# Splitting each streamed weight slot into its high and low parts with one instruction of 1024 columns per engine instead of two of 512

## The chip, the cores and the metric

One NeuronCore of a Trainium2 chip runs the whole program. The metric is the device time of one execution in microseconds (us), as the median of several executions of the same program on the same inputs. Lower is better. Engines are named as in the profile: PE is TensorE (the matmuls), PEld its weight loads, DVE is VectorE, ACT is ScalarE, POOL is GpSimd, SP is SyncE, whose queue issues the weight loads.

## The reference

A two layer trunk over 512 latent tokens and 256 context tokens of width 1024, batch 1. Both layers share the same frame:

```python
hl = rmsnorm(x, norm_g[i]) * (1.0 + sc_l) + sh_l        # modulation from silu(c) @ ada_w[i]
# layer 0 (also for the context tokens)
u, z = split(h @ w_in, 2)                               # (tokens, 1024) @ (1024, 4096)
y = fft2(u grouped by 256 features, axes=(tokens, features), norm='ortho').real
x = x + gate * ((y * silu(z)) @ w_out)                  # (tokens, 2048) @ (2048, 1024)
# layer 1, four heads, latent and context tokens
q, k, v, z = split(h @ w_in)                            # q, k rotated for the latent tokens
o = forward + backward retention (decayed scores, state from the context)
x = x + gate * ((rms(o) * silu(z)) @ w_out)
return rmsnorm(x, final_g)
```

Everything is float32.

## The kernel before, in words

**Precision and the split.** Each float32 operand a of a large matmul is used as two numbers: a high part, which is a copy of a into the type fp32r, and a low part, a minus the high part. A product is then three matmuls, high by high, high by low and low by high (`mm3`, lines 1541 to 1543), added in PSUM. So each weight must be split before PE can use it: ACT writes the high part (`hi`, line 662), DVE the low part (`lo`, line 1003).

**The stream.** All large weights lie in DRAM in the order of their use, in slots of 128 by 1024 float32 numbers (512 KB). SP loads them into `raw`, two or three buffers by stage. `ring` holds the split form and has two slots: slot r goes to `ring[:, r % 2]`, its high part at index 0, its low part at index 1.

**The protocol around a slot, half by half.** A slot has two halves of 512 columns. Three counters tie the engines together, each counting two per slot:
- `slot_done` is counted up by PE after the last matmul that reads a half. ACT waits for it before it overwrites this half with the high part of the slot after next.
- `hi_done` is counted up by ACT for each half; DVE waits for it.
- `split_done` is counted up by DVE for each half; PE waits for it (`split`) ahead of the first matmul that reads the half, and SP waits for both halves of a slot before it loads into that slot's `raw` buffer again.

So as soon as PE has finished half 0 of slot r-2, ACT and DVE can split half 0 of slot r, while PE works on half 1.

**Order.** There is no scheduler. Each engine executes one instruction list in order, written out by hand, in which `hi` and `lo` stand between the other work of that stage. A waiting instruction holds up all that follows it on its engine.

**Stages that use `hi` and `lo`**, 96 slots in all:
- z (16 slots of 48 matmuls): the gate projection of layer 0. Between them DVE takes dot products with the streamed modulation weights (line 1035) and POOL multiplies the gates (line 585). The slots of stage u before it are split by `fold_hi` and `fold_lo`, which the change leaves as they are.
- out0 (16 slots of 48): the output projection of layer 0, then the norm of layer 1, where DVE makes 1/rms (1321, 1343), scales (1328) and takes low parts of the activations (1334).
- four heads of 12 slots, s0 to s11: s0, s1 are q, s2, s3 and s6, s11 are z, s4, s5 are k, s7 to s10 are v. Within a head DVE rotates q and k (1393) from PSUM into `turn`, POOL adds up pairs of these (633, 635), ACT and DVE split the sums (893, 1397). DVE and ACT also split v out of PSUM (926, 1449), and the last head's output is normed (1351, 1358) and gated by POOL (625) between the next head's first slots.
- out1 (16 slots of 24): the output projection of layer 1.

On ACT and DVE, `used(s)` in the function `head` is the split of slot s+2, so `used(1)` splits s3 and `used(2)` splits s4. For heads 1 to 3 DVE's order begins

```python
used(0)
o_rstd(h - 1)
used(1)
turns(0, 0, 1)
o_norm(h - 1, 0, 2)
part_lo(1, ...); part_lo(2, ...)
o_norm(h - 1, 2, 4)
used(2)
```

and ahead of s7 PE waits for `turned` and `qklo`, both counted by DVE's work on k, which stands behind `used(5)`, the split of s7. Ahead of s11 PE waits for `vlo`: its PSUM bank 0 holds a tile of v until DVE has taken the low part of it (1449). This stands behind `used(10)`, the split of the next head's s0.

Of the kernel before, what the change touches and what calls it, by code (L numbers as in the profile page):

```python
# [30 lines left out]
ALU = mybir.AluOpType  # L31
ACT = mybir.ActivationFunctionType
# [19 lines left out]
SLOT = 1024  # L52
# [22 lines left out]
DONE0 = 4  # L75
# [12 lines left out]
def raw_at(phase, n):  # L88

    _, bufs, first, before = PHASES[phase]  # L90
    buf = (n + first) % bufs
    return buf, 16 * (before[buf] + n // bufs + 1)


def raw_step(phase, per_iteration):

    return 16 * (per_iteration // PHASES[phase][1])
# [58 lines left out]
def build(nc, x_lat, x_ctx, x_rows, small_in, cond_in, decay_in, stream, tables_in, middle_in,  # L156
          middle_w_in, rope_in, out):
    ctx = ExitStack()
    with ctx:
        def sb(name, shape, dt=F32):  # L160
            return ctx.enter_context(nc.sbuf_tensor(name, shape, dt))

        def sem(name):
            return ctx.enter_context(nc.semaphore(name))


        ring = sb("ring", [P, 2, 2, SLOT], F32R)
# [6 lines left out]
        raw = sb("raw", [P, RAW_BUFS, SLOT])  # L174
# [20 lines left out]
        def f32(ap):  # L195
            return ap.bitcast(F32)
# [129 lines left out]
        hi_done, split_done, slot_done = sem("hi_done"), sem("split_done"), sem("slot_done")  # L326
# [327 lines left out]
        def _(act):  # L654
            def hi(phase, n, r, i=0, per=0):

                buf, landed = raw_at(phase, n)
                act.wait_ge(s_raw[buf], raw_step(phase, per) * i + landed if per else landed)
                for a in range(2):
                    c = slice(a * SLOT // 2, (a + 1) * SLOT // 2)  # L660
                    act.wait_ge(slot_done, 2 * r + (a + 1 - 4 + DONE0))
                    act.activation(ring[:, n % 2, 0, c], raw[:, buf, c], ACT.Copy).then_inc(hi_done, 1)  # L662

            def fold_hi(n):

# [79 lines left out]
            for g in range(GROUPS):  # L745
                if g >= 1:
                    u_hi(g - 1)
                if g >= 2:
                    copy_q(g - 2)
                if g < GROUPS - 1:  # L750
                    fold_hi(2 * g + 2)
                    fold_hi(2 * g + 3)
                else:
                    hi("z", 0, SLOT_Z)
                    hi("z", 1, SLOT_Z + 1)
                if g == 0:
                    act.wait_ge(mid_mm, 1)
                    act.activation(mid_s[0][0:GROUPS, :], bank(7, NF, parts=GROUPS),
                                   ACT.Copy).then_inc(mid_s_hi, 1)
                    act.wait_ge(rstd_row_mm, 1)  # L760
                    act.activation(rstd0, banks[:, 4 * 512:4 * 512 + TOK], ACT.Copy).then_inc(rstd_row, 1)
# [12 lines left out]
            def gates(jj, q, split=None, first=False, last=False):  # L774

                j = 2 * jj + q
                if split is not None:
                    act.wait_ge(gated, 8 * split + 8)
                    for half in range(2):
                        act.activation(g0_hi_at(2 * split + half), one(gate0, 2 * split + half),  # L780
                                       ACT.Copy).then_inc(ghi, 1)
                if last:
                    hi("out0", 0, RING_OUT0)
                    hi("out0", 1, RING_OUT0 + 1)
                else:
                    hi("z", Z_PER * q + 4, 2 * j + (SLOT_Z + 2), jj, 2 * Z_PER)
                    if first:
                        copy_q(GROUPS - 1)
                    hi("z", Z_PER * q + 7, 2 * j + (SLOT_Z + 3), jj, 2 * Z_PER)
                for half in range(2):  # L790
                    for a, b, src in ((0, LAT, bank(3 * q + half)),
                                      (LAT, TOK, bank(3 * q + 2, CTX, CTX * half))):
                        kk = 2 * j + half if split is not None else gate0_at(2 * j + half)
                        act.activation(one(gate0[:, :, a:b], kk), src, ACT.Silu).then_inc(z_done, 1)  # L794
# [193 lines left out]
        def _(dve):  # L988
# [8 lines left out]
            def lo(phase, n, r):  # L997

                buf = raw_at(phase, n)[0]
                for a in range(2):  # L1000
                    c = slice(a * SLOT // 2, (a + 1) * SLOT // 2)
                    dve.wait_ge(hi_done, 2 * r + (a + 1))
                    dve.tensor_tensor(ring[:, n % 2, 1, c], raw[:, buf, c],  # L1003
                                      f32(ring[:, n % 2, 0, c]), ALU.subtract).then_inc(split_done, 1)

            def fold_diff(n):

# [188 lines left out]
            for g in range(GROUPS):  # L1196
                if g < GROUPS - 1:
                    fold_diff(2 * g + 2)
                    fold_diff(2 * g + 3)
                if g >= 1:  # L1200
                    u_lo(g - 1)
                if g >= 2:
                    sum_diff(g - 2)
                if g < GROUPS - 1:
                    fold_lo(2 * g + 2)
                    fold_lo(2 * g + 3)
                else:
                    lo("z", 0, SLOT_Z)
                    lo("z", 1, SLOT_Z + 1)
                if g == 0:  # L1210
                    dve.wait_ge(mid_s_hi, 1)
                    dve.tensor_tensor(mid_s[1][0:GROUPS, :], bank(7, NF, parts=GROUPS),
                                      f32(mid_s[0][0:GROUPS, :]), ALU.subtract).then_inc(mid_s_lo, 1)
# [8 lines left out]
            def gates(jj, q, split=None, first=False, last=False):  # L1222
# [20 lines left out]
                if last:  # L1243
                    dot(2, 4)
                    dot(3, 5)
                    keep_dots(j + EARLY, Z_PER * j + (SLOT_Z + 5))
                    lo("out0", 0, RING_OUT0)
                    lo("out0", 1, RING_OUT0 + 1)
                else:
                    lo("z", Z_PER * q + 4, 2 * j + (SLOT_Z + 2))  # L1250
                    dot(2, 5)
                    dot(3, 6)
                    keep_dots(j + EARLY, Z_PER * j + (SLOT_Z + 6))
                    lo("z", Z_PER * q + 7, 2 * j + (SLOT_Z + 3))
# [744 lines left out]
```

## Time and profile before

| what | value |
|---|---|
| median of 3 runs | 1000.4 us |
| those runs | 1000.3, 1000.4 and 2994.8 us |
| the profiled execution's own time | 998.61 us |
| its span, first to last instruction | 996.8 us |
| mean granted TensorE clock | 0.978 of full speed |
| PE busy | 941.6 us, 94% of the span |
| DVE busy | 562.2 us, 56% |
| ACT busy | 343.6 us, 34% |
| POOL busy | 248.3 us, 25% |
| bytes moved | 98.67 MB, 99 GB/s on average |

The profiled execution is 1.8 us (0.2%) below the median of the timed ones, and 1.8 us of it lie outside the span. PE's 94% is a mean over all stages; the busy share alone doesn't tell where it waits or how near to waiting it is.

### The profile page before, as it was taken

What the parts mean: (1) busy time and instruction counts of PE and PEld (TensorE: products, weight loads), DVE (VectorE), ACT (ScalarE), POOL (GpSimd) and SP (SyncE); (2) the same over time, 40 slices, a digit from 0 to 9 for tenths busy, and PEclk for the clock granted to TensorE, in tenths of its full rate; (3) what the DMA queues carried; (4) which work ended last, traced back from release to release, by engine and by line L of the source; (5) the groups of instructions that cost most, each with busy time, mean ns of one, the idle gap of its engine ahead of it and who ended that gap; (6) DMA issues with size and microseconds to landing.
All of it is one profiled execution on the core that took longest, in us unless ns stands there. A gap on an engine that the chain in (4) does not pass through costs nothing.

```text
span 996.8 us, 12904 instructions
## 1 busy us (share of the span) xinstructions
PE 941.6 (94%) x4748; PEld 810.4 (81%) x4748; DVE 562.2 (56%) x804; ACT 343.6 (34%) x577; POOL 248.3 (25%) x244
## 2 busy tenths in 40 slices
PE   6969998999999999959999999999999999998993
PEld 6968998888888888847888888887888788877882
DVE  6485877899995332358334445426434544565344
ACT  7233334232314332334333334323333323452230
POOL 3337970475574000024100131013100410020001
PEclk9989999999999999989999999999999999998997
DMA  8473332555555211211221122202121121102212
GB/s 307 140 233 152 121 101 90 190 191 173 186 188 206 92 64 64 84 42 56 72 76 52 35 72 69 68 13 84 63 65 40 42 84 42 63 1 89 101 63 84
DMA packets 27864, 98.67 MB, mean 99 GB/s; under 512 B 3848, under 2 KB 4008, under 8 KB 27568
## 3 DMA queue, kind: packets, MB, share of 16 engines
q1 hardware_dynamic: 25792, 90.25, 27.1%
q0 software_dynamic: 2032, 7.89, 2.1%
q8 instruction: 24, 0.39, 0.2%
q14 instruction: 16, 0.13, 0.0%
HBM read 96.01 MB, written 2.10 MB: 98 GB/s over the span
## 4 chain that ended last, share of the span: by engine, by line
PE 87%; DVE 7%; DMA 2%; POOL 2%; ACT 1%; issue 1%; DVEq 0%; SPq 0%; POOLq 0%
PE banks L1541 28%; PE banks L1542 28%; PE banks L1543 27%; DMA raw<-stream 2%; PE banks L1594 2%; DVE hreg L1334 1%; POOL gate L625 1%; DVE xreg L1393 1%; DVE gate L1328 1%; DVE ring L1003 1%; DVE xreg L1533 0%; DVE gate L1358 0%; POOL gate L618 0%; POOL xreg L635 0%; PE banks L1783 0%
## 5 line engine op out<-in xcount | busy, mean ns | idle before, releaser
L1541 PE MATMUL banks<-hreg,ring 128*128 128x512 f32 (+2 forms) x928 | 334.1, 360 | 26.9 <-DVE hreg L1334 9.1
L1542 PE MATMUL banks<-hreg,ring 128*128 128x512 f32 (+2 forms) x928 | 331.8, 358 | 0.0
L1543 PE MATMUL banks<-hreg,ring 128*128 128x512 f32 (+2 forms) x928 | 329.2, 355 | 0.0
L1003 DVE TENSOR_TENSOR ring<-raw,ring 128x512 fp32r<-128x512 f32 x192 | 139.9, 745 | 271.5 <-ACT ring L662 270.8
L662 ACT ACTIVATE ring<-raw 128x512 fp32r<-128x512 f32 x192 | 119.3, 630 | 386.6 <-PE banks L1543 304.7
L1541 PEld LDWEIGHTS banks<-hreg,ring 128*128 128x128 f32 x928 | 176.6, 190 | 55.4 <-issue 12.8
L1543 PEld LDWEIGHTS banks<-hreg,ring 128*128 128x128 f32 x928 | 176.1, 190 | 23.3
L1542 PEld LDWEIGHTS banks<-hreg,ring 128*128 128x128 f32 x928 | 176.6, 190 | 22.3 <-issue 1.0
L585 POOL TENSOR_TENSOR gate<-xreg,gate 128x257 f32<-128x257 f32 (+1 forms) x64 | 76.1, 1219 | 74.0 <-ACT gate L794 57.9
L1035 DVE CUSTOM_DVE_ANT_0 dist<-raw,gate 128x1024 bf16<-128x1024 f32 x64 | 85.8, 1341 | 3.8
L618 POOL TENSOR_TENSOR gate<-gate 128x512 f32<-128x512 f32 x12 | 16.8, 1397 | 250.7 <-ACT gate L868 249.9
L1541 PE MATMUL banks<-ring,hreg 128*128 128x512 f32 x192 | 74.7, 389 | 0.0
L1542 PE MATMUL banks<-ring,hreg 128*128 128x512 f32 x192 | 74.7, 389 | 0.0
L1543 PE MATMUL banks<-ring,hreg 128*128 128x512 f32 x192 | 74.7, 389 | 0.0
L1541 PE MATMUL banks<-wreg 128*128 128x512 f32 (+2 forms) x192 | 72.4, 377 | 0.0
L1543 PE MATMUL banks<-wreg 128*128 128x512 f32 (+2 forms) x192 | 71.9, 375 | 0.0
L1542 PE MATMUL banks<-wreg 128*128 128x512 f32 (+2 forms) x192 | 71.9, 374 | 0.0
L1542 PE MATMUL banks<-wreg,ring 128*128 128x512 f32 (+2 forms) x168 | 58.5, 348 | 0.0
L1543 PE MATMUL banks<-wreg,ring 128*128 128x512 f32 (+2 forms) x168 | 58.1, 346 | 0.0
L1541 PE MATMUL banks<-wreg,ring 128*128 128x512 f32 (+2 forms) x168 | 57.8, 344 | 0.0
L1541 PEld LDWEIGHTS banks<-ring,hreg 128*128 128x128 f32 x192 | 36.0, 188 | 7.5
L1542 PEld LDWEIGHTS banks<-ring,hreg 128*128 128x128 f32 x192 | 36.0, 188 | 7.5
(205 smaller groups left out, 1117.5 us busy)
## 6 DMA issues: line engine op xcount, KB each, us to landing
raw<-stream SPq DMA_DIRECT2D x160, 512.0 KB, 3.3
gate<-x_rows SPq DMA_DIRECT2D x6, 512.0 KB, 6.8
gate<-x_lat POOLq DMA_DIRECT2D x1, 2048.0 KB, 9.5
xreg<-x_lat POOLq DMA_DIRECT2D x1, 2048.0 KB, 10.9
out<-xreg SPq DMA_DIRECT2D x5, 256.0 KB, 2.7
gate<-cond_in POOLq DMA_DIRECT2D x2, 512.0 KB, 4.9
gate<-x_ctx POOLq DMA_DIRECT2D x1, 1024.0 KB, 12.1
xreg<-x_ctx POOLq DMA_DIRECT2D x1, 1024.0 KB, 13.7
```

The costliest lines, as they stand in the source:

```text
L585: pool.tensor_tensor(g, y, g, ALU.mult).then_inc(gated, 1)
L618: pool.tensor_tensor(head_rstd, head_rstd, p_f[:, i % 2, :], ALU.add).then_inc(oacc, 1)
L625: pool.tensor_tensor(g, g, p_f[:, i % 2, :], ALU.mult).then_inc(ogated, 1)
L662: act.activation(ring[:, n % 2, 0, c], raw[:, buf, c], ACT.Copy).then_inc(hi_done, 1)
L1003: dve.tensor_tensor(ring[:, n % 2, 1, c], raw[:, buf, c], f32(ring[:, n % 2, 0, c]), ALU.subtract).then_inc(split_done, 1)
L1035: dve.tensor_tensor_reduce(out=dot_out, in0=raw[:, buf, :], in1=cond_rows[:, v, :], scale=1.0, scalar=0.0, op0=ALU.mult, op1=ALU.add, accu ...
L1328: dve.tensor_tensor(tmp_t[:, k, 0:LAT], tmp_t[:, k, 0:LAT], rstd_t[:, 0:LAT], ALU.mult).then_inc(t_vec, 1)
L1334: dve.scalar_tensor_tensor(out=h_lo[:, k, a:b], in0=tmp_t[:, k, a:b], scalar=mod1[:, 8 + k, v:v + 1], in1=f32(h_hi[:, k, a:b]), op0=ALU.ad ...
L1541: pe.matmul(out, left[0], right[0], start=start, stop=False)
L1542: pe.matmul(out, left[0], right[1], start=False, stop=False)
L1543: return pe.matmul(out, left[1], right[0], start=False, stop=stop)
L1594: last = pe.matmul(o, raw[:, buf, P * k:P * k + P], csf[:, k:2 * KT:KT], start=k == 0, stop=k == KT - 1)
```

## The change

ACT's copy and DVE's subtraction for a streamed slot each become one instruction over all 1024 columns. ACT waits until PE has read both halves of the slot after which this place in the ring comes free, and counts `hi_done` up by two. DVE waits for both, and counts `split_done` up by two. PE's waits, SP's waits, the loads and the slots of stage u are as before.

```diff
                 buf, landed = raw_at(phase, n)
                 act.wait_ge(s_raw[buf], raw_step(phase, per) * i + landed if per else landed)
-                for a in range(2):
-                    c = slice(a * SLOT // 2, (a + 1) * SLOT // 2)
-                    act.wait_ge(slot_done, 2 * r + (a + 1 - 4 + DONE0))
-                    act.activation(ring[:, n % 2, 0, c], raw[:, buf, c], ACT.Copy).then_inc(hi_done, 1)
+                act.wait_ge(slot_done, 2 * r + (2 - 4 + DONE0))
+                act.activation(ring[:, n % 2, 0, :], raw[:, buf, :], ACT.Copy).then_inc(hi_done, 2)
...
                 buf = raw_at(phase, n)[0]
-                for a in range(2):
-                    c = slice(a * SLOT // 2, (a + 1) * SLOT // 2)
-                    dve.wait_ge(hi_done, 2 * r + (a + 1))
-                    dve.tensor_tensor(ring[:, n % 2, 1, c], raw[:, buf, c],
-                                      f32(ring[:, n % 2, 0, c]), ALU.subtract).then_inc(split_done, 1)
+                dve.wait_ge(hi_done, 2 * r + 2)
+                dve.tensor_tensor(ring[:, n % 2, 1, :], raw[:, buf, :], f32(ring[:, n % 2, 0, :]),
+                                  ALU.subtract).then_inc(split_done, 2)
```

## Rows read from the trace of the kernel before

**Rows 1.** The page: busy time of each engine; the chain that ended last, by engine.
```profile
PE 941.6 (94%) x4748; PEld 810.4 (81%) x4748; DVE 562.2 (56%) x804; ACT 343.6 (34%) x577; POOL 248.3 (25%) x244
...
PE 87%; DVE 7%; DMA 2%; POOL 2%; ACT 1%; issue 1%; DVEq 0%; SPq 0%; POOLq 0%
```

**Rows 2.** Waits of PE: for whom, us in total, times, longest.
```profile
PE banks L1541 <- DVE hreg L1334: 9.1, 4, 7.9
...
PE banks L1541 <- DVE ring L1003: 7.6, 5, 4.4
PE banks L1541 <- DVE hreg L1219: 2.6, 1, 2.6
```

**Rows 3.** The two edited lines by source: ns minimum/median/maximum of one; 1024-column forms elsewhere.
```profile
L662 ACT ACTIVATE ring<-raw x192: 614/632/645, 151.9 to 968.0; 128x512 fp32r<-128x512 f32 x192
...
L1003 DVE TENSOR_TENSOR ring<-raw,ring x192: 626/692/1776, 152.6 to 968.7; 128x512 fp32r<-128x512 f32 x192
...
L690 ACT ACTIVATE wreg<-gate x5: 1042/1043/1057, 12.5 to 21.2; 128x1024 fp32r<-128x1024 f32 x5
...
L1092 DVE TENSOR_TENSOR wreg<-gate,wreg x5: 1212/1218/1218, 16.1 to 26.2; 128x1024 fp32r<-128x1024 f32 x5
```

**Rows 4.** Timeline, head 1, slots s3 and s4: start, us, instruction, [idle before].
```profile
569.51 0.63 ACT L662 ACTIVATE ring<-raw 128x512 fp32r<-128x512 f32 x1 [2.10 <-PE banks L1543]
...
570.18 0.69 DVE L1003 TENSOR_TENSOR ring<-raw,ring 128x512 fp32r<-128x512 f32 x1 [0.17 <-ACT ring L662]
570.79 2.48 DVE L1393 TENSOR_TENSOR xreg<-banks,gate 128x512 f32<-128x512 f32 x4
...
573.34 1.30 POOL L633 TENSOR_TENSOR xreg<-xreg 128x512 f32<-128x512 f32 x1 [10.08 <-DVE xreg L1393]
...
575.34 2.81 DVE L1397 TENSOR_TENSOR wreg<-xreg,wreg 128x512 fp32r<-128x512 f32 x2 [0.88 <-ACT wreg L893]
...
579.34 0.69 DVE L1358 TENSOR_TENSOR gate<-banks,gate 128x512 f32<-128x512 f32 x1 [0.59 <-POOL gate L625]
579.94 2.85 DVE L1003 TENSOR_TENSOR ring<-raw,ring 128x512 fp32r<-128x512 f32 x2
...
579.25 1.30 POOL L625 TENSOR_TENSOR gate<-gate 128x512 f32 x1
...
580.50 1.74 POOL L625 TENSOR_TENSOR gate<-gate 128x512 f32 x1
...
581.15 0.50 PE L1541 MATMUL banks<-hreg,ring 128*128 128x512 f32 x1 [0.80 <-DVE ring L1003]
```

**Rows 5.** Timeline, head 0 to head 1, around slot s11.
```profile
528.48 0.69 DVE L1003 TENSOR_TENSOR ring<-raw,ring 128x512 fp32r<-128x512 f32 x1 [3.33 <-ACT ring L662]
529.09 2.48 DVE L1449 TENSOR_TENSOR wreg<-banks,wreg 128x512 fp32r<-128x512 f32 x4
...
530.33 0.39 PE L1541 MATMUL banks<-hreg,ring 128*128 128x512 f32 x1
```

**Rows 6.** Timeline, head 0, around slot s7.
```profile
490.38 0.69 DVE L1003 TENSOR_TENSOR ring<-raw,ring 128x512 fp32r<-128x512 f32 x1 [3.45 <-ACT ring L662]
...
493.71 0.41 DVE L1397 TENSOR_TENSOR wreg<-banks,wreg 128x256 fp32r<-128x256 f32 x1
...
494.97 0.39 PE L1541 MATMUL banks<-ring,hreg 128*128 128x512 f32 x1
```

**Rows 7.** Timeline, the start of stage z; a window behind it, PEclk after POOL.
```profile
158.87 0.69 DVE L1003 TENSOR_TENSOR ring<-raw,ring 128x512 fp32r<-128x512 f32 x1 [1.38 <-ACT ring L662]
...
162.53 0.47 PE L1541 MATMUL banks<-hreg,ring 128*128 128x512 f32 x1 [2.60 <-DVE hreg L1219]
...
162.60:166.00 3.40, 3.40 (x20) 2.96 (x21) 3.40 (x5) 3.40 (x6) 0.00 (x0) 1.00 0.02 5
```

**Rows 8.** Timeline, the first slot of out0.
```profile
296.69 1.16 ACT L662 ACTIVATE ring<-raw 128x512 fp32r<-128x512 f32 x2 [12.02 <-DMA raw<-stream]
...
297.42 1.29 DVE L1003 TENSOR_TENSOR ring<-raw,ring 128x512 fp32r<-128x512 f32 x2 [0.71 <-ACT ring L662]
...
299.12 0.40 PE L1541 MATMUL banks<-wreg,ring 128*128 128x512 f32 x1
```

**Rows 9.** Timeline, from out0 to head 0, and slot s2 of head 0.
```profile
434.50 0.63 ACT L819 ACTIVATE gate<-xreg 128x512 f32<-128x512 f32 x1 [0.16 <-DVE xreg L1289]
...
460.98 0.68 DVE L1003 TENSOR_TENSOR ring<-raw,ring 128x512 fp32r<-128x512 f32 x1
...
461.72 0.50 PE L1541 MATMUL banks<-hreg,ring 128*128 128x512 f32 x1 [0.73 <-DVE ring L1003]
```

**Rows 10.** Timeline, from head 3 to out1; then a window at the next stretch: PEclk is after POOL.
```profile
899.30 1.28 DVE L1003 TENSOR_TENSOR ring<-raw,ring 128x512 fp32r<-128x512 f32 x2
...
900.03 0.80 PE L1541 MATMUL banks<-hreg,ring 128*128 128x512 f32 x1 [4.42 <-DVE ring L1003]
...
900.00:905.00 5.00, 4.97 (x12) 3.95 (x13) 4.19 (x7) 0.04 (x1) 0.00 (x0) 0.50 0.60 191
```

**Rows 11.** Timeline, last slot of out1; then the page's DMA issues, us to landing.
```profile
968.66 0.69 DVE L1003 TENSOR_TENSOR ring<-raw,ring 128x512 fp32r<-128x512 f32 x1 [1.97 <-ACT ring L662]
...
973.23 0.39 PE L1541 MATMUL banks<-hreg,ring 128*128 128x512 f32 x1
...
raw<-stream SPq DMA_DIRECT2D x160, 512.0 KB, 3.3
```

## The prediction

> **What bounds the kernel now.** I read the page first: PE is busy for 94% of the span and holds 87% of the chain that ended last [rows 1]. ACT and DVE, the two engines that the change edits, have half their time and more to spare, so nothing that merely shortens their work shows in the total. The second view is the list of PE's waits: in the part of the run that the change touches, PE waits for DVE's work on activations, for 7.6 us in five places for a split slot, and for 2.6 us at the start of stage z [rows 2]. The third is the timeline around each of these places, and around those where PE only just doesn't wait. The question is no longer how much ACT and DVE do, but how soon after PE lets go of a half the next instruction behind the split can run.
>
> **The price of one slot.** A half costs ACT 0.632 us and DVE 0.692 us; the same operations at 1024 columns, from the start of this kernel, cost 1.043 and 1.218 [rows 3]. So the change takes 2 x 0.632 - 1.043 = 0.22 us per slot from ACT and 2 x 0.692 - 1.218 = 0.17 us from DVE, 21 and 16 us over 96 slots. Most of that is overlap of neighbouring instructions anyway: back to back, DVE starts one every 0.61 us (570.18 to 570.79 in [rows 4]), so I take 1.218 - 0.08 = 1.14 us for the whole against 1.22 for two. The saving in sequence is then 0.08 us per slot. All of this is beside PE's matmuls, and I cost it at nothing.
>
> What counts is the handover. Let PE have read half 1 of slot r-2, and ACT start at once. Before, half 0 has long been split, and DVE is free for its next work 0.63 + 0.04 + 0.61 = 1.28 us after ACT's start (569.51, 570.18, 570.79 in [rows 4]; 0.04 us is the semaphore between them). After, it is free 1.04 + 0.04 + 1.14 = 2.22 us after it. So whatever stands behind a split that waits for PE comes 0.94 us later on DVE, and 1.04 - 0.63 = 0.41 us later on ACT. And where PE waits for half 0 alone, it now waits for 1.21 instead of 0.68 us of DVE.
>
> In most of the 96 slots this is covered: PE has a whole slot of at least 24 matmuls between its release and its first read of slot r. In stage out1, where slots are shortest, both halves are ready at 969.35 and read from 973.23, a cover of 3.88 us [rows 11]; after the change 2.9 would be left. The cover fails at these places:
>
> - **s4 of heads 1 to 3.** PE's release of s1 lets ACT start at 569.51. ACT and DVE split half 1 of s3, and right behind this DVE turns q; then POOL adds, ACT and DVE split q, DVE norms the last head's output in step with POOL's gating, and only then splits s4, for which PE already waits 0.80 us today [rows 4]. Every link follows the one before at once, so 0.94 us go through to the split of s4: it starts at 580.88. At that time POOL's third gating (579.26 to 580.56 before) will still run, and the fourth follows it. In these rows DVE's first half ends at 581.10, 0.54 us after the end of the third, though it started at 579.94, and the second at 582.79, 0.55 us after the end of the fourth. So I take it that the whole waits for the end of the third, at 580.56 + 0.94 = 581.50, and then needs 0.54 + 0.53 = 1.07 us: 582.57, and PE goes at 582.62 instead of 581.15. That is 1.47 us per head, 4.4 for three. The bounds are 1.0 us (a whole of 1.22 us without a collision) and 2.6 (both collisions stay, 2.85 us), so 3.0 to 7.8.
> - **s11 of all four heads.** DVE splits half 1 of the next head's s0 at 528.48 and starts on v at 529.09; PE needs the first low part of v, which ends 0.68 later at 529.77, before s11 at 530.33 [rows 5]. 0.56 us of cover against 0.94 of delay, and 0.04 for the semaphore: 0.42 per head, 1.7 in all. Bounds 1.4 and 2.0.
> - **s7 of all four heads.** Here k's work stands behind the split of s7, and ends at 493.71 + 0.41 = 494.12; PE goes on at 494.97 [rows 6]. Cover 0.85, delay 0.94, semaphore 0.04: 0.13 per head, 0.5 in all, between 0 and 1.0.
> - **Start of z.** DVE's split of the second slot stands ahead of its work on u and of the first low part of h, for which PE waits until 162.53 [rows 7]. No cover: 0.95 us. The bounds are 0.8 and 1.0.
> - **First slot of out0.** ACT starts on the landing of the load at 296.69, DVE ends at 298.71 and PE reads at 299.12 [rows 8], without waiting. After, the split ends 1.04 + 0.04 + 1.22 = 2.30 us after ACT's start, at 298.99, which would still do. But DVE is filled up through stage z, and two splits there, whose high part comes only at PE's release, would hold it 0.4 us longer, and the load with it. 0.3 us, between 0 and 0.7.
> - **From out0 to head 0.** ACT's copy for s1 ends 0.41 us later, at 434.75, and the first square of the last tile, on the way to 1/rms, starts then instead of 434.50: 0.27 us [rows 9]. Then s2: DVE reaches it at 460.98 with its high part ready, and PE goes at 461.72, after half 0. After, it goes after the whole, 1.218 - 0.68 = 0.53 us later. Together 0.8, between 0.5 and 1.0. What is late next is DVE's turn of q in head 0, and this is not late: the two splits ahead of it fill DVE either way.
> - **Third slot of out1.** The same: DVE comes to it at 899.30, PE goes at 900.03 [rows 10]: 0.5 us, between 0.4 and 0.7.
>
> SP's queue waits for the end of both halves before and after, so its loads start 0.94 us later where the split waits for PE; its loads land in some 3.3 us [rows 11], ahead of ACT's next wait for PE in out0, out1 and the heads. I cost this at nothing; if that cover were gone it would be up to 0.9 us per slot.
>
> The sum: 4.4 + 1.7 + 0.5 + 0.95 + 0.3 + 0.8 + 0.5 = 9.2 us, with ends at 6.1 (3.0 + 1.4 + 0 + 0.8 + 0 + 0.5 + 0.4) and 14.2 (7.8 + 2.0 + 1.0 + 1.0 + 0.7 + 1.0 + 0.7). The profiled execution took 998.61 us, so it becomes 1007.8. The median of the runs is 1000.4, 1.8 above it; by the same sum it becomes 1009.6.
>
> A port shared by DVE and POOL is what these rows suggest for s4. The Trainium skill states this as a rule (page SBUF — State Buffer, section Who interferes with whom): a VectorE instruction with two SBUF inputs contends with a GpSimd one that reads SBUF, and whoever comes first holds the pair for its whole instruction. By that rule DVE waits once, for the third gating, and s4 costs the 1.47 us that I took; were there no such rule it would be 1.0, and the sum 7.8 us.
>
> **The rivals.**
>
> *Fewer instructions win, the covers hold.* The saved 0.08 us of sequence per slot would count wherever DVE is the bound, and if DVE's 0.94 us were absorbed in the links to s4 (a wait there that is really someone else's, as POOL's or ACT's), that chain would shorten: two splits per transition, 0.16 us for each of three, and one split ahead of each of PE's four other waits for DVE behind a split, 0.3 us, 0.8 in all: 999.6. It decides at whether DVE's turns really start at the end of the split of s3. Against it: the turns start 0.61 us after the split, with no idle time listed between them [rows 4]. The Trainium skill speaks for this rival (page Advanced Engine Details and Errata, section The Read-Write Bubble): on ScalarE and VectorE a latency is exposed between instructions, and it advises tiles of 512 or 1024 elements. The durations agree, 1.218 against 2 x 0.692 us; the rule says nothing of what waits for the whole. Chance 0.07.
>
> *Only the present waits grow.* PE's five waits for a split slot [rows 2] get the 0.53 us of a longer first handover, the chain to s4 gets its 0.95 without more loss to POOL, and s7 and s11 stay covered, should DVE's and PE's order there leave more room than the rows of heads 0 and 1 show: 3 x 1.0 + 0.95 + 0.5 + 0.5, about 5 us: 1005.4. Chance 0.13. Against it the arithmetic of 0.56 us of cover at s11.
>
> *The clock falls once more.* After PE's wait of 4.42 us ahead of 900.03 the granted clock stands at half for the next 5 us [rows 10], that is at 1.2 GHz, which costs 2.5 us of PE. PE's wait of 2.60 us at the start of z has no such stretch behind it, the clock there stays full, at 2.4 GHz [rows 7]. After the change that wait is 3.5 us, between the two, and the ones at s4 are 2.3, still below. If one more fall comes, the time is 1009.6 + 2.5, about 1012; if the clock fell at the three transitions too, 1009.6 + 4 x 2.5 = 1019.6. Chance of the one 0.2, of the other 0.03.
>
> *The change doesn't do what it says.* Nothing keeps the halves apart any more, so this could only be a wait that I misread. I give it no share.
>
> **How the numbers follow.** Forecast 0.57, at 1009.6, its own range 1006.5 to 1014.6 by the ends of the sum; the rivals 0.07 at 999.6, 0.13 at 1005.4, 0.2 at 1012 and 0.03 near 1019. A range from 1004.6 to 1014.2 leaves out the first and the last of the rivals and the tails of the sum. A difference of 2% (20 us) is about what a measurement of this kernel can tell from no change; a loss of that size needs the clock to fall in all places and more, a gain of it is excluded, since PE alone is busy for 941.6 us and all its waits for split slots are 7.6. So: faster 0.01, within 2% 0.95, slower 0.04.
>
> **What would show each step.** The two edited lines should have 96 instructions each, near 1.04 and 1.22 us, the latter longer where POOL is at work. In the list of PE's waits, those for DVE's split should grow from 7.6 to about 13.5 us, the one for the first low part of h from 2.6 to 3.55, and new ones should appear for the low part of v (four times, 0.4 us each) and of k (four times, 0.1). DVE's turns in heads 1 to 3 should start 2.22 us after ACT's copy for s3 instead of 1.28. The granted clock after the start of z tells of the third rival. I am wrong if DVE's work behind a split doesn't move with it, or if a cover that I read from one head is different in the others.

## The result, and the profile after

The changed kernel is slower: 1017.84 us in the median of 4 runs (1016.03 to 1021.38), against 1001.22 for the kernel before in its 4 runs (1000.3, 1000.4, 1002.05 and one of 2994.8). The ratio is 1.0164, with a 95% interval of 1.0136 to 1.0192, which is within the 2% to which the forecast gave a chance of 0.95. The prediction was 1009.6 us with a range of 1004.6 to 1014.2, so the direction was right, the size was too small by nearly half, and the time lies 3.6 us above the range. A second measurement with more runs is among the experiments; it gives 1.0149 (1.0123 to 1.0175), 15.5 us.

The page of the kernel after, with the lines that answer to those of before: busy time by engine, the granted clock in 40 slices, the chain by engine, and the two edited lines.

```profile
span 1019.6 us, 12756 instructions
...
PE 956.5 (94%) x4748; PEld 821.2 (81%) x4748; DVE 548.0 (54%) x708; ACT 326.7 (32%) x481; POOL 254.1 (25%) x244
...
PEclk9779998999999999989999999999999999998997
...
PE 84%; DVE 9%; POOL 2%; ACT 2%; DMA 1%; issue 1%; DVEq 0%; SPq 0%; ACTq 0%; POOLq 0%
...
L999 DVE TENSOR_TENSOR ring<-raw,ring 128x1024 fp32r<-128x1024 f32 x96 | 122.2, 1276 | 313.1 <-ACT ring L660 312.7
L660 ACT ACTIVATE ring<-raw 128x1024 fp32r<-128x1024 f32 x96 | 101.7, 1059 | 413.4 <-PE banks L1539 392.8
```

ACT has 17 us less to do and DVE 14, as the change intends, and neither was needed. DVE's share of the chain went up from 7% to 9% [rows 1]: it works less and is waited for more. PE is busy for 15 us more with the same 4748 matmuls, which is the mark of a lower clock: 6.8 of these 15 us lie ahead of stage z, which the change doesn't touch (27.3 us at half clock there instead of 13.7), and 8.1 behind it.

The waits of PE in the kernel after (for whom, us in total, times, longest):

```profile
PE banks L1537 <- DVE ring L999: 13.4, 5, 4.9
PE banks L1537 <- DVE hreg L1330: 8.8, 3, 7.9
...
PE banks L1537 <- DVE hreg L1215: 3.6, 1, 3.6
...
PE banks L1537 <- DVE wreg L1445: 2.0, 4, 0.5
PE banks L1537 <- DVE wreg L1393: 0.7, 3, 0.2
```

The waits for a split slot were 7.6 us and are 13.4, the one at the start of z was 2.6 and is 3.6 [rows 2]. Those for the low parts of v (L1445, ahead of s11) and of k (L1393, ahead of s7) are new.

The timeline of the kernel after at head 1, s3 and s4, in the columns of [rows 4]:

```profile
580.12 1.06 ACT L660 ACTIVATE ring<-raw 128x1024 fp32r<-128x1024 f32 x1 [3.27 <-PE banks L1539]
...
581.28 1.23 DVE L999 TENSOR_TENSOR ring<-raw,ring 128x1024 fp32r<-128x1024 f32 x1 [1.05 <-ACT ring L660]
582.42 0.68 DVE L1389 TENSOR_TENSOR xreg<-banks,gate 128x512 f32<-128x512 f32 x1
...
590.96 0.69 DVE L1354 TENSOR_TENSOR gate<-banks,gate 128x512 f32<-128x512 f32 x1 [0.58 <-POOL gate L625]
591.56 1.67 DVE L999 TENSOR_TENSOR ring<-raw,ring 128x1024 fp32r<-128x1024 f32 x1
...
590.89 1.26 POOL L625 TENSOR_TENSOR gate<-gate 128x512 f32 x1
...
593.29 0.79 PE L1537 MATMUL banks<-hreg,ring 128*128 128x512 f32 x1 [2.39 <-DVE ring L999]
```

DVE's turn of q starts 2.30 us after ACT's copy (580.12 to 582.42), where it was 1.28. The split of s4 starts at 591.56, while POOL's third gating runs until 592.15, and ends 1.08 us after that, at 593.23. So the chain to s4 is as forecast. The matmul behind it takes 0.79 us instead of 0.50, and that was not in the forecast's sum: a stretch at half clock begins at the same time, at 593.29.

Such stretches show in windows of the same trace around the end of PE's wait at z and behind its waits at s4 in heads 1, 2 and 3. The columns are PE, PEld, DVE, ACT and POOL busy, then the granted clock, the DMA share and GB/s:

```profile
166.70:173.40 6.70, 5.46 (x16) 4.62 (x17) 6.70 (x9) 4.02 (x6) 0.00 (x0) 0.50 0.18 68
...
593.40:596.60 3.20, 3.20 (x9) 2.68 (x10) 2.05 (x1) 1.05 (x2) 0.97 (x1) 0.50 0.52 164
...
706.00:709.30 3.30, 3.01 (x9) 2.52 (x10) 2.46 (x2) 1.43 (x3) 1.37 (x1) 0.50 0.51 158
819.20:822.50 3.30, 3.30 (x19) 2.91 (x20) 2.14 (x1) 1.11 (x3) 1.06 (x1) 1.00 0.52 160
```

At half clock, 1.2 GHz, PE does 9 matmuls in heads 1 and 2 in the time in which it does 19 in head 3 (2.4 GHz), whose wait was as long (2.41 us, against 2.39 and 2.41).

### The profile page after: what moved, and what is told of

Same layout as the page of the kernel before. It is cut to its first block, busy times and chain, and to the rows that moved or that the text cites. A ratio compares the mean times of both kernels' runs of the same rounds, so it can differ in the third digit from the quotient of the medians.

```text
span 1019.6 us, 12756 instructions
## 1 busy us (share of the span) xinstructions
PE 956.5 (94%) x4748; PEld 821.2 (81%) x4748; DVE 548.0 (54%) x708; ACT 326.7 (32%) x481; POOL 254.1 (25%) x244
## 4 chain that ended last, share of the span: by engine, by line
PE 84%; DVE 9%; POOL 2%; ACT 2%; DMA 1%; issue 1%; DVEq 0%; SPq 0%; ACTq 0%; POOLq 0%
PE banks L1537 27%; PE banks L1538 27%; PE banks L1539 26%; PE banks L1590 3%; DVE ring L999 2%; DVE xreg L1389 1%; DMA raw<-stream 1%; ACT ring L660 1%; DVE hreg L1330 1%; POOL gate L625 1%; DVE gate L1324 1%; DVE xreg L1529 0%; PE banks L1610 0%; POOL gate L618 0%; POOL xreg L635 0%
## 5 line engine op out<-in xcount | busy, mean ns | idle before, releaser
L1537 PE MATMUL banks<-hreg,ring 128*128 128x512 f32 (+2 forms) x928 | 337.6, 364 | 33.3 <-DVE ring L999 13.4
L999 DVE TENSOR_TENSOR ring<-raw,ring 128x1024 fp32r<-128x1024 f32 x96 | 122.2, 1276 | 313.1 <-ACT ring L660 312.7
L660 ACT ACTIVATE ring<-raw 128x1024 fp32r<-128x1024 f32 x96 | 101.7, 1059 | 413.4 <-PE banks L1539 392.8
L1537 PEld LDWEIGHTS banks<-hreg,ring 128*128 128x128 f32 x928 | 178.7, 193 | 63.9 <-DVE ring L999 18.3
L1539 PEld LDWEIGHTS banks<-hreg,ring 128*128 128x128 f32 x928 | 177.9, 192 | 23.6
L1538 PEld LDWEIGHTS banks<-hreg,ring 128*128 128x128 f32 x928 | 178.7, 193 | 22.6 <-issue 1.0
L585 POOL TENSOR_TENSOR gate<-xreg,gate 128x257 f32<-128x257 f32 (+1 forms) x64 | 82.5, 1318 | 72.3 <-ACT gate L792 55.2
L1031 DVE CUSTOM_DVE_ANT_0 dist<-raw,gate 128x1024 bf16<-128x1024 f32 x64 | 90.4, 1412 | 3.8
L1537 PE MATMUL banks<-wreg 128*128 128x512 f32 (+2 forms) x192 | 73.3, 382 | 0.0
L1538 PE MATMUL banks<-wreg 128*128 128x512 f32 (+2 forms) x192 | 72.6, 378 | 0.0
L1539 PE MATMUL banks<-wreg 128*128 128x512 f32 (+2 forms) x192 | 72.6, 378 | 0.0
L633 POOL TENSOR_TENSOR xreg<-xreg 128x512 f32<-128x512 f32 x8 | 10.3, 1284 | 138.3 <-DVE xreg L1389 138.3
L1537 PEld LDWEIGHTS banks<-ring,hreg 128*128 128x128 f32 x192 | 36.0, 188 | 9.9 <-issue 1.9
```

The costliest lines, as they stand in the source:

```text
L585: pool.tensor_tensor(g, y, g, ALU.mult).then_inc(gated, 1)
L633: pool.tensor_tensor(turn[0], turn[0], turn[1], ALU.subtract).then_inc(summed, 1)
L660: act.activation(ring[:, n % 2, 0, :], raw[:, buf, :], ACT.Copy).then_inc(hi_done, 2)
L999: dve.tensor_tensor(ring[:, n % 2, 1, :], raw[:, buf, :], f32(ring[:, n % 2, 0, :]), ALU.subtract).then_inc(split_done, 2)
L1031: dve.tensor_tensor_reduce(out=dot_out, in0=raw[:, buf, :], in1=cond_rows[:, v, :], scale=1.0, scalar=0.0, op0=ALU.mult, op1=ALU.add, accu ...
L1537: pe.matmul(out, left[0], right[0], start=start, stop=False)
```

## The experiments

PE's waits from stage z to the end are the measure that doesn't move with the clock: I add up the gaps between the matmuls in each trace. They come to 24.0 us in the kernel before and 34.2 in the changed one. What the clock does shows in a second measure, the time from the first matmul of z to the end of the span: 834.3 us before (996.8 - 162.5), 851.7 in the changed kernel (1019.6 - 167.9). It leaves out the stages ahead of z, whose length changes from one execution to the next.

**The changed kernel again.** No edit.

> The changed kernel once more, beside the kernel before on one chip. My theory: 10.2 us of the loss are longer waits of PE at 14 places (s4, s7, s11, start of z, first slots of out0, head 0 and out1), and these are the same in every execution; the rest is the granted clock, which falls to half for more stretches than before. So PE's waits from stage z on should come out at 34.2 us again within 0.3, while the total may move by several us with the clock: 1014 to 1021 us, a ratio of 1.013 to 1.019. The part of the profiled run ahead of stage z, which the change doesn't touch, was 4 us longer than before, with 27 us at half clock against 14. If this is chance it should be different this time; a rival, that the program's other length or layout slows its start, says that it stays at 4 us.

1017.56 us in the median of 6 runs, ratio 1.0149 (1.0123 to 1.0175), waits from z on 34.6 us, 0.4 above the first profile where I allowed 0.3. The part ahead of z is now 0.4 us longer than in the first profile of before, not 4, so the length of that part is chance and no slower start of this program. From z's first matmul to the end it is 851.7 us again. The kernel before, too, spread from 998.55 to 1006.61 us over 17 runs on this chip, with a median of 1002.03; the run on which my sum stood, 998.61, was one of its fastest.

I compared the starts of all 4748 matmuls of this trace with those of before. The span is 18.9 us longer, and this is all of it: 0.4 ahead of z; 1.0 of wait and 2.5 of half clock at z; 0.9 at the first slot of out0; 0.25 at 1/rms and 0.6 at s2 of head 0; 2.0 at the four s7; 3.1 at the four s11; 4.8 at the three s4, and 1.4 and 1.6 of half clock behind two of them; 0.4 in out1.

**Whole where covered, whole where tight.** The 24 slots that I had found tight keep their halves, in `hi` as in `lo`; the second kernel has `in HALVED` for `not in HALVED`. The entry for slot 2 of out1 stands in a loop and takes in slots 6 and 10 as well, so it is 26 slots against 70 in both kernels, and not 24 against 72 as the expectations say (ACT's copies of 1024 columns: 70 in the first trace, 26 in the second):

```diff
+HALVED = {("z", 1), ("out0", 0), ("head", 1), ("head", 2), ("head", 3), ("head", 4), ("head", 7),
+          ("head", 12), ("out1", 0), ("out1", 2)}
...
+                if (phase, n) not in HALVED:
+                    act.wait_ge(slot_done, 2 * r + (2 - 4 + DONE0))
+                    act.activation(ring[:, n % 2, 0, :], raw[:, buf, :], ACT.Copy).then_inc(hi_done, 2)
+                else:
+                    for a in range(2):
...
```

> Whole instructions in 72 of the 96 slots, halves as before in the 24 for which the trace shows too little cover (second slot of z, first of out0, s1 ahead of head 0, s2, s3, s4, s7 of each head, s0 of the next, slots 0 and 2 of out1). My theory, the handover at tight places: PE's waits from z on as before, 24.0 us, and the time of the kernel before within 2 us (ratio 0.998 to 1.002). Rival, the wide instruction itself costs (its hold of the port shared with POOL, its separate semaphore instructions): three quarters of the loss stay, about 1013 us.

Waits 24.0 us; 1003.41 us, ratio 1.0001 (0.9983 to 1.0020) in 12 runs. 70 whole splits cost nothing and gain nothing, within 2 us.

> The complement: whole instructions in those 24 slots alone, halves in the other 72. Handover theory: PE's waits from z on 34 us, as in the changed kernel, and its time, 1014 to 1020. Rival of the wide instruction itself: a quarter of the loss, about 1005.

Waits 34.9 us; 1021.20 us, ratio 1.0186 (1.0156 to 1.0216), which is above the 1014 to 1020 expected. It is 3.6 us more than the changed kernel took beside it, but the intervals overlap and from z's first matmul to the end its trace has 851.2 us, nearly the changed kernel's 851.7. These 26 carry the loss. The rival of a costly wide instruction falls with both runs. The waits of PE in the first and then in the second kernel:

```profile
PE banks L1555 <- DVE ring L1017: 7.6, 5, 4.4
...
PE banks L1555 <- DVE hreg L1233: 2.6, 1, 2.6
```

```profile
PE banks L1555 <- DVE ring L1011: 13.4, 5, 5.0
...
PE banks L1555 <- DVE hreg L1233: 3.6, 1, 3.6
...
PE banks L1555 <- DVE wreg L1463: 2.0, 4, 0.5
PE banks L1555 <- DVE wreg L1411: 0.7, 3, 0.3
```

The first list is that of the kernel before, to the tenth; the second is that of the changed one. One place is in neither: the changed kernel's wait ahead of the first slot of out0 (0.41 us, 0.64 in the second profile), which so needs whole splits in stage z and in this slot together. The second kernel has 0.9 to 1.2 us more of waits for the norm of layer 1 instead (10.0 in L1348, against 8.8 and 9.1 in the two profiles of the changed kernel), so that the two sums agree so closely is in part luck.

**Only s3 whole** (`if (phase, n) == ("head", 3):` in both functions).

> Whole only in s3 of each head (4 slots of 96). My theory: DVE's turn of q comes 1.05 us later (0.94 and two times 0.06 for the semaphore instructions) and s4 with it, so that PE waits 0.8 + 1.0 = 1.8 us ahead of s4 in heads 1 to 3 instead of 0.8, and nowhere else longer; 3 us in all, about 1004, if the clock doesn't fall. Rival, that it is the split of s4 itself which costs at s4: PE's wait stays at 0.8 us.

One run, 1004.53 us, where about 1004 was expected if the clock doesn't fall; it fell once behind s4, in head 2, for 3.4 us. The timeline of this kernel at s4 of head 1:

```profile
584.11 0.50 PE L1550 MATMUL banks<-hreg,ring 128*128 128x512 f32 x1 [1.86 <-DVE ring L1012]
```

1.86 us, and 1.87 and 1.89 in the other heads: 1.06 more than before, by a split that isn't the one waited for. The other 0.53 up to 2.39 belong to the width of s4 itself.

**Halves, both late; DVE alone; ACT alone.** In the first, ACT's copies stay two but both wait for the release of the whole slot. The other two kernels take one of the change's two functions each.

```diff
-                    act.wait_ge(slot_done, 2 * r + (a + 1 - 4 + DONE0))
+                    act.wait_ge(slot_done, 2 * r + (2 - 4 + DONE0))
```

> Two instructions of 512 columns per engine as before, but ACT waits for PE's release of the whole slot ahead of both; DVE and PE still go by halves. It keeps the later start and takes away the width. By the handover theory DVE is free 0.63 + 0.04 + 2 x 0.61 = 1.89 us after ACT's start instead of 1.28, so 0.61 us later and not 1.05 as in the changed kernel: PE waits 0.8 + 0.6 = 1.4 us ahead of s4, 3.2 at the start of z, 0.05 to 0.1 at s11, none at s7, 0.73 at s2 of head 0 and 4.4 in out1, 24.0 + 3.1 = 27 us from z on; time 1005 or 1006, a ratio of 1.003 to 1.005. Rival, that the late start is all and the width nothing: 34 us and 1017.

> ACT by halves, each as soon as PE has released it; DVE whole. Handover theory: DVE starts 0.63 + 0.10 us after ACT's start on half 1 (0.06 of it for a separate semaphore instruction) and is free 1.14 later, 1.87 instead of 1.28. So 0.6 us through to s4, then 0.53 more since PE waits for the whole of s4: 0.8 + 1.15 = 1.95 us ahead of s4, 3.2 at z, 0.1 at s11, none at s7, 1.26 at s2 of head 0. Rival, that ACT's wait for the whole is what costs: as in the kernel before.

> The complement of the run with DVE whole: ACT whole, DVE by halves. Handover theory: DVE starts 1.04 + 0.04 (and 0.06 for ACT's semaphore instruction) after PE's release and is free 2 x 0.61 later, so 2.36 us instead of 1.28 + 0.04: PE waits 0.8 + 1.08 = 1.9 us ahead of s4, 3.65 at z, 0.5 at s11, 0.2 at s7, but 0.73 at s2 of head 0 and 4.4 in out1, since PE still goes after DVE's first half. Rival, that DVE's width alone is the cause: the waits of the kernel before.

> ACT whole, DVE by halves, once more, since the execution before ran with all matmuls at some 0.73 us, which tells nothing of waits of 1 us. As before: PE waits 1.9 us ahead of s4, 3.65 at z, 0.5 at s11, 0.2 at s7, but 0.73 at s2 of head 0 and 4.4 in out1. Rival, that DVE's width alone is the cause: the waits of the kernel before.

The first run of ACT alone took 2418.66 us, with PE busy for 98% of the span and matmuls of 512 columns of 0.83 us instead of 0.39; it tells nothing about waits of 1 us, so the kernel was run again: 1017.9 us, in one run. Halves late took 1008.81, ratio 1.0062 (1.0036 to 1.0088), 3 us more than expected though its waits are as expected; DVE alone 1007.84, in one run. PE's wait in us at each place, all from the traces, those of the changed kernel from its first one:

| | before | halves late | DVE whole | ACT whole | changed |
|---|---|---|---|---|---|
| start of z | 2.60 | 3.18 | 3.12 | 3.63 | 3.63 |
| s2 of head 0 | 0.73 | 0.68 | 1.24 | 0.72 | 1.26 |
| s7, each | 0 | 0 | 0 | 0.21 to 0.23 | 0.21 to 0.24 |
| s11, each | 0 | 0 to 0.08 | 0 | 0.44 to 0.53 | 0.44 to 0.53 |
| s4, heads 1 to 3 | 0.80 | 1.38 to 1.44 | 1.92 to 1.94 | 1.87 to 1.88 | 2.39 to 2.41 |
| slot 2 of out1 | 4.42 | 4.40 | 4.97 | 4.45 | 4.92 |
| all waits from z on | 24.0 | 27.5 | 28.9 | 32.3 | 34.2 |
| z's first matmul to the end | 834.3 | 839.6 | 842.4 | 847.8 | 851.7 |

The expected waits hold to about 0.1 us. The parts are now apart: the start at the release of the whole slot costs 0.6 us at z and at s4, where the chain to PE's wait runs through the split; ACT's instruction of 1024 columns makes this 1.03 and 1.07, and with it the waits at s7 and s11 open; DVE's width costs 0.5 to 0.55 wherever PE used to go after the first half (s2, s4, out1). DVE whole with ACT's halves on time still loses 0.5 at z, since DVE can start only after ACT's second half. So ACT's side alone, with its late start and its width, brings 8.3 of the 10.2 us of added waits, and DVE's side alone 4.9; part of the two is the same delay.

**PE kept busy.** Matmuls of no use, of 512 columns into a bank that is free, in PE's list ahead of its waits; first in the changed kernel, at z (14) and at s4 (10), then in the kernel before, at all its waits over 0.7 us from z on.

```diff
+            split(SLOT_Z, 1)
+            fill(14, bank(7), ring[:, 0, 0, 0:P], ring[:, 0, 0, 0:512])
             pe.wait_ge(u_lo_done, 2 * GROUPS)
...
+                    pe.wait_ge(turned, 8 * h + 4)
+                    fill(10, bank(0), h_hi[:, 0, 0:P], h_hi[:, 0, 0:LAT])
                     pe.wait_ge(onorm, 4 * h)
```

> The changed kernel, with matmuls of no use in PE's list: 14 of 512 columns ahead of stage z into a free bank, 10 ahead of s4 in heads 1 to 3. They fit into waits of 3.6 and 2.4 us (0.21 us each) and change no wait of another engine. Theory of the clock: the half-clock stretches after the start of z and after s4 (6.9 and 3.4 us in the last profile) come from PE's longer idle times, so they vanish, and the time falls by 2 to 5 us against the changed kernel's 1017.6, to about 1014, ratio 1.011. Rival, that the clock falls by chance and not for these waits: stretches as before and 1017 to 1018.

The half-clock stretches at these places are gone; elsewhere some stay (13.7 us at the norm of layer 1 and 3.4 at out1's wait, 10.2 and 6.8 in both profiles of the changed kernel). Windows of this kernel behind the start of z and behind s4 in heads 1 to 3, with the clock at 1.00 and 18 to 20 matmuls each:

```profile
169.90:173.00 3.10, 3.10 (x18) 2.70 (x19) 3.10 (x4) 2.78 (x4) 0.00 (x0) 1.00 0.03 5
...
593.00:596.30 3.30, 3.30 (x19) 2.89 (x20) 2.06 (x1) 1.03 (x2) 0.97 (x1) 1.00 0.54 164
704.50:707.80 3.30, 3.30 (x19) 2.90 (x20) 2.08 (x1) 1.04 (x2) 1.00 (x1) 1.00 0.47 169
816.00:819.30 3.30, 3.30 (x19) 2.90 (x20) 2.10 (x1) 1.07 (x2) 1.02 (x1) 1.00 0.51 168
```

The time, 1016.06 us, ratio 1.0137 (1.0112 to 1.0163), is 1.5 us below the changed kernel's, where I expected 2 to 5. The intervals overlap, so the timing alone doesn't prove the gain. From z's first matmul to the end this trace has 845.7 us, 5.9 less than both traces of the changed kernel (851.7). Against the second of these, 2.6 of them are saved between z and s2 of head 0, 1.3 and 1.5 behind the two s4 that had a stretch there, and the rest in out1. Its part ahead of z was 2 us longer than in the longer of those two, which hides some of this in the time. That such stretches are gone at all four places, and in the next kernel at every wait from z on, ties them to PE's idle time and not to chance.

> The kernel before, with such matmuls in all waits of PE of over 0.7 us from z on: 9 ahead of z, 8 and 31 around 1/rms of layer 1, 3 ahead of s4, 17 in out1. Theory of the clock: the stretch after out1's wait, 6.8 us, vanishes and gives back 2.5 us; the one in head 0, 10.2 us, vanishes too but gives back little, since DVE's 1334 sets the pace there; one after z, where there is one, as well. So 2.5 to 4 us faster than the kernel before, ratio 0.996 to 0.9975. Rival, chance: 1.000.

998.84 us in 12 runs, ratio 0.9971 (0.9952 to 0.9990): 3.2 us faster than the kernel before, within the 2.5 to 4 expected. From z to the last wait no stretch at half clock is left in its trace. Where the kernel before stood at half clock for 5 us in out1 [rows 10], this one has:

```profile
904.30:909.30 5.00, 5.00 (x22) 4.15 (x23) 4.60 (x8) 0.63 (x1) 0.00 (x0) 1.00 0.60 180
```

**Counting by one per slot.** In the heads and out1, `then_inc(hi_done, 1)` and `then_inc(split_done, 1)` for a whole slot, with the waits renumbered.

> The changed kernel, with the counters hi_done and split_done counted up by one per slot instead of two in the heads and out1. In the changed kernel each handover takes 0.10 us where it took 0.04 before, and the profile shows a semaphore instruction of its own ahead of the copy and of the subtraction, which the kernel before has not. Theory: an instruction that counts up by more than one can't carry its wait. Counting by one then gives back 2 x 0.06 us per handover: PE's waits at s7 fall from 0.23 to 0.11 us and at s11 from 0.52 to 0.40, at s4 from 2.40 to 2.28, 1.3 us in all; time about 1016, ratio 1.013 to 1.015. Rival, that the longer gap belongs to the 1024 columns: waits as in the changed kernel.

The waits at s7 fell to 0.09 to 0.15 us, at s11 to 0.35 to 0.43, at s4 to 2.28 to 2.33, each by about 0.1 as expected, so the longer handover comes from the count and not from the columns. Here the handover from ACT to DVE takes 0.04 us (577.02 + 1.06 = 578.08 to 578.12), against 0.10 in the changed kernel (580.12 + 1.06 = 581.18 to 581.28):

```profile
577.02 1.06 ACT L663 ACTIVATE ring<-raw 128x1024 fp32r<-128x1024 f32 x1 [3.28 <-PE banks L1544]
...
578.12 1.23 DVE L1004 TENSOR_TENSOR ring<-raw,ring 128x1024 fp32r<-128x1024 f32 x1 [0.98 <-ACT ring L663]
```

The traces bear out the separate semaphore instructions: DVE executes 91 semaphore instructions in all in the kernel before and with ACT alone whole, 183 in the changed kernel. The time, 1019.07 us, ratio 1.0152 (1.0114 to 1.0191), lies above the 1016 expected and can't tell 1.3 us from none; the clock fell behind all three s4 here.

## Why the prediction was wrong

**The direction, the places and the chain were right.** All seven places where I saw too little cover are those that cost, and the comparison of all matmuls and the kernel with 70 whole splits show no eighth. The saving on ACT and DVE is worth nothing where the split is covered, as costed. The rival that fewer instructions win falls with it; so does the one of only the present waits, since s7 and s11 did open.

**Two terms failed: the clock, which the sum put at nothing, and the size of s7 and s11.** The steps of the sum, against what the second trace of the changed kernel shows:

| step | forecast, us | measured, us |
|---|---|---|
| s4, three heads | 4.4 | 4.8 |
| s11, four heads | 1.7 | 3.1 |
| s7, four heads | 0.5 | 2.0 |
| start of z | 0.95 | 1.0 |
| first slot of out0 | 0.3 | 0.9 |
| 1/rms and s2 of head 0 | 0.8 | 0.8 |
| slot 2 of out1 | 0.5 | 0.4 |
| sum of the waits | 9.2 | 13.0 |
| half clock at z and behind s4 | 0; as rivals 2.5 with chance 0.2, and 10 with 0.03 | 5.4 in this trace |

With 13.0 instead of 9.2 us of waits the sum gives 1000.4 + 13.0 = 1013.4 us, still inside the range; with the clock it leaves it.

**The clock.** I set "one more fall" beside the forecast with a chance of 0.2, and took the waits of 2.3 us at s4 to be safe because one of 2.60 us had no such stretch behind it. That single row was a weak bound. In the two profiles of the changed kernel the clock fell at z both times, and behind four of six waits of 2.4 us at s4; in other profiles it fell at the wait of 2.60 at z as well (in the kernel with 70 whole splits a stretch begins at 166.5, where PE's wait of 2.60 ends at 166.83; with s3 alone whole one begins there too). Of the nine waits of 1.86 to 1.94 us at s4 (s3 alone, DVE alone, ACT alone) four had a fall behind them. So a wait of this length may or may not cost a fall. The case that the traces come nearest to is the rival of falls at z and all three transitions, 1019.6 us, to which I gave 0.03: three of its four falls came, in each trace. The price of 2.5 us was right for the long stretch at z, 2.45 us, and too high for a short one behind s4, 1.4 and 1.6. In the mean over runs the clock's share is less than in these traces: with the waits at 13.0 and the measured loss at 15.5 us, some 2.5 us are left for it, and the busy PE gave back 1.5. The kernel before has falls at z too in part of its executions, as the two kernels with its wait of 2.60 suggest; no run measures how often.

**The size of s7 and s11.** I took a new wait's price as its overhang: 0.13 and 0.42 us. Measured are 0.5 and 0.8, together 5.1 us instead of 2.2. Two things are missing in the working. DVE is free 0.12 us later than I had it, because counting up by two puts a semaphore instruction ahead of both operations; the run with a count of one shows this. And in the trace, where the ends of matmuls are modelled, a matmul starts while the one before it still runs; where PE didn't wait before, a wait costs this overlap too, and a longer first matmul. The timeline of the changed kernel at s11 of head 0, and two matmuls from the steady run behind it:

```profile
538.87 1.22 DVE L999 TENSOR_TENSOR ring<-raw,ring 128x1024 fp32r<-128x1024 f32 x1 [6.93 <-ACT ring L660]
540.01 1.28 DVE L1445 TENSOR_TENSOR wreg<-banks,wreg 128x512 fp32r<-128x512 f32 x2
...
540.75 0.50 PE L1537 MATMUL banks<-hreg,ring 128*128 128x512 f32 x1 [0.44 <-DVE wreg L1445]
...
544.96 0.39 PE L1537 MATMUL banks<-hreg,ring 128*128 128x512 f32 x1
545.18 0.39 PE L1538 MATMUL banks<-hreg,ring 128*128 128x512 f32 x1
```

In the steady run one starts 0.22 us after the other and takes 0.39, an overlap of 0.17. At s11 the list says 0.44 us; the matmul starts 0.83 us after its predecessor, where it was 0.23, so 0.60 later, and with its 0.50 us and those behind it the place loses 0.74. At s4 and z, where PE had waited already, this term is not in the difference, and the forecast there holds to 0.15 us each. The first slot of out0, 0.3 against 0.9, is a new wait of the same kind.

**Smaller things.** The median of the three runs shown, 1000.4, lies 1.6 us below that of 17 later ones; this base has no part in the ratio, which is 1.015 without it. The 0.27 us at 1/rms is 0.25 by its own rows (434.50 to 434.75). And the 13.5 us foretold for the list of waits for a split doesn't follow from the terms, which give 7.6 + 4.4 + 0.5 + 0.5 = 13.0; that 13.4 came is in part the 0.12 us of each s4 that the sum didn't have.

**The port shared by DVE and POOL.** At s4 of head 1 there was one wait, to the end of the third gating, and the split ended 1.08 us behind it, as [rows 4] suggested; the fourth gating, started at 592.11, then took 2.26 us and ended 1.13 us behind the split. The rule of the Trainium skill (page SBUF — State Buffer, section Who interferes with whom) says this, that the instruction which comes first has the shared pair and the other waits, and this trace agrees with it. In all s4 cost 1.59 to 1.61 us against 1.47. What lies above is the semaphore instructions of s3: with a count of one it was 1.48 to 1.53.

## What to carry to other kernels

Before two small steps are merged into a large one, look at what follows the step on its own engine and at who waits for its first half: the merged step's saving counts only where that engine is the bound, its later end counts wherever the cover is shorter than the delay, and one list of these places predicts the loss. Here 70 of 96 merges were free and 26 carried some 15 us; the same list says which may be merged. A wait that lengthens on TensorE must be priced with its overlap and with the chance of a clock fall behind it. A few matmuls of no use in waits that can't be removed were worth 3 us of 1002 here, where the merge could gain nothing.

## What the runs showed of the hardware that I had not expected

- In this kernel a copy or subtraction that counts a semaphore up by two had a separate semaphore instruction for its wait ahead of it: 0.10 us from ACT's end to DVE's start instead of 0.04; with a count of one it was 0.04 again.
- The granted clock fell to half, for 3.4 us at s4, behind some of PE's waits of 1.9 to 2.6 us and not behind others of the same length, at s4 even in the same trace. With these waits filled with matmuls of no use, no fall came at any of them.
- Executions of one unchanged kernel lie up to 8 us apart (998.55 to 1006.61), and the part ahead of stage z was 4 us longer in the first profile of the changed kernel than in the second, with 27.3 us at half clock instead of 17.1 (13.7 in the profile of the kernel before).
- One execution took 2418.66 us, with matmuls of 512 columns of 0.83 us instead of 0.39. Its trace holds no record of the granted clock, so whether that was the clock stays open.
